# Moving the first products of a projection one pair of tiles earlier in the order of TensorE

## The reference

```python
h = rmsnorm(x, norm_mix[l])                    # x * rsqrt(mean(x*x) + eps) * g
proj = jnp.einsum('bsd,de->bse', h, w_in[l])   # [2048, 1024] x [1024, 2312]
# ... swa_sink_attention, forgetting_attention, w_out, residual, MLP, final norm
```

## Time and profile before

| what | value |
| --- | --- |
| median of 3 runs | 2398.11 us (2395.19 to 2401.05) |
| profiled execution, its time | 2394.05 us |
| its span | 2392.4 us |
| TensorE busy | 2326.6 us, 97% of the span |
| VectorE busy | 1520.1 us, 64% |
| ScalarE busy | 1154.1 us, 48% |
| GpSimd busy | 706.9 us, 30% |
| mean granted TensorE clock | 0.995 |

### The profile page before, as it was taken

One profiled execution on the slowest core, in us unless ns is written; L12 is line 12 of the kernel. 1 busy time (PEld: TensorE's weight loads), 2 busy tenths in 40 slices (PEclk: granted clock), 3 DMA queues, 4 the chain that ended last, 5 costly groups with the idle time before them and its releaser, 6 DMA issues.

```text
span 2392.4 us, 34959 instructions
## 1 busy us (share of the span) xinstructions
PE 2326.6 (97%) x11346; PEld 1934.7 (81%) x11346; DVE 1520.1 (64%) x2623; ACT 1154.1 (48%) x2226; POOL 706.9 (30%) x593
## 2 busy tenths in 40 slices
PE   7999999999999998999899999999999999999998
PEld 5888888788888886887687877888888888888887
DVE  6588873688888886566745655444465555564454
ACT  5211112788888886223545555555553233333243
POOL 2000000111111114235568764666640032120132
PEclk9999999999999999999999999999999999999999
DMA  5567765666666565766455576654457486564464
GB/s 189 215 235 278 268 242 163 180 160 156 160 157 157 152 156 169 248 218 202 170 183 163 189 286 242 202 160 152 154 190 260 165 298 234 193 219 162 138 219 160
DMA packets 253970, 469.09 MB, mean 196 GB/s; under 512 B 59336, under 2 KB 119752, under 8 KB 246032
## 3 DMA queue, kind: packets, MB, share of 16 engines
q1 hardware_dynamic: 247808, 451.11, 58.6%
q0 software_dynamic: 6048, 16.52, 2.6%
HBM read 316.13 MB, written 151.42 MB: 195 GB/s over the span
## 4 chain that ended last, share of the span: by engine, by line
PE 51%; DVE 3%; POOL 2%; issue 2%; DMA 1%; ACT 1%; SPq 0%; POOLq 0%; ACTq 0%; DVEq 0%
PE m_ps L2533 24%; PE m_ps L2556 23%; PE m_ps L1685 4%; DMA b_kept<-f_kept 1%; POOL m_mix L1548 1%; DVE f_up_lo L2389 1%; PE m_ps L2574 0%; DVE m_xn L1653 0%; DVE m_xm L1646 0%; DVE m_mix L1622 0%; ACT m_mix_hi L1585 0%; DVE keep_lo L2408 0%; POOL h_raw L1560 0%; POOL f_kept L2157 0%; DVE hop_lo L1659 0%
## 5 line engine op out<-in xcount | busy, mean ns | idle before, releaser
L2556 PE MATMUL m_ps<-keep_hi,hop_hi 128*128 128x512 f32 x880 | 342.5, 389 | 0.4 <-DVE hop_lo L2392 0.4
L2556 PE MATMUL m_ps<-keep_hi,hop_lo 128*128 128x512 f32 x880 | 342.4, 389 | 0.0
L2556 PE MATMUL m_ps<-keep_lo,hop_hi 128*128 128x512 f32 x880 | 342.3, 389 | 0.0
L2392 DVE TENSOR_TENSOR hop_lo<-h_raw,hop_hi 128x512 fp32r<-128x512 f32 x224 | 176.6, 789 | 236.8 <-ACT hop_hi L2228 236.7
L2389 DVE TENSOR_TENSOR f_up_lo<-wide_raw,f_up_hi 128x512 fp32r<-128x512 f32 x160 | 182.5, 1142 | 223.0 <-ACT f_up_hi L2223 222.9
L2228 ACT ACTIVATE hop_hi<-h_raw 128x512 fp32r<-128x512 f32 x224 | 140.8, 630 | 334.4 <-PE m_ps L2556 330.5
L958 POOL DMA_DIRECT2D o_main<-a_o x63 | 36.5, 580 | 775.2 <-ACT a_o L1326 726.6
L599 PE MATMUL p_ps_o<-p_ht_lo,p_w_hi 128*128 128x512 f32 x576 | 224.5, 390 | 0.0
L2533 PE MATMUL m_ps<-keep_hi,f_up_hi 128*128 128x512 f32 x512 | 202.8, 396 | 6.1 <-DVE f_up_lo L2389 4.7
L2533 PE MATMUL m_ps<-keep_hi,f_up_lo 128*128 128x512 f32 x512 | 201.3, 393 | 0.0
L2533 PE MATMUL m_ps<-keep_lo,f_up_hi 128*128 128x512 f32 x512 | 199.4, 390 | 0.0
(11 more groups left out here) (246 smaller groups left out, 5779.8 us busy)
## 6 DMA issues: line engine op xcount, KB each, us to landing
h_raw<-u_ops SPq DMA_DIRECT2D x224, 256.0 KB, 4.2
wide_raw<-in_w_up SPq DMA_DIRECT2D x32, 1024.0 KB, 7.2
u_ops<-f_u SPq DMA_DIRECT2D x128, 256.0 KB, 4.3
wide_raw<-in_x SPq DMA_DIRECT2D x59, 512.0 KB, 4.0
u_ops<-f_us SPq DMA_DIRECT2D x96, 256.0 KB, 2.3
proj_hi<-p_o_hi SPq DMA_DIRECT2D x17, 1024.0 KB, 6.2
proj_lo<-p_o_lo SPq DMA_DIRECT2D x17, 1024.0 KB, 8.3
h_raw<-in_w_down SPq DMA_DIRECT2D x58, 256.0 KB, 3.9
```

The lines of the kernel that those rows point to most:

```text
L2392: nc.vector.tensor_tensor(lo, a_raw[:, (m - UP) % A_RING], hi.bitcast(F32), ALU.subtract).then_inc(op_lo_done, 1)
L2556: last = nc.tensor.matmul(down_banks[b % 2][t][:], a[:, cols], w[j], start=(j == 0 and m == 0), stop=(j == FG - 1 and m == 2))
```

## The change

It does five things. `product_after_turn` becomes 3, 5, 7, 9, 11, 13 and 15 for products 0 to 6, and only product 7 stands behind all turns. `product_first(0)` asks for the low part of the first chunk's weights alone, and the others for both. On ScalarE the squares of tiles 1 to 4 are done one tile earlier relative to the high parts (squares of later tiles stay where they were), and the first two chunks' weight splits, which stood together behind tile 2, stand behind tiles 2 and 3. On VectorE the weight splits are parted likewise, and the norm of tile 4 moves behind the low part of tile 3 and the second weight split. `GATE_TILE` becomes 5. The unused squared values, which went into half of `p_o_hi0`, go into the last 256 columns of each of four pieces of `keep_hi`, where tiles 14 and 15 come later, so the wait for all squares moves from `split_first(4)` to `split_ht_hi(14)`.

```diff
-        squares = whole.raw["p_o_hi0"][:, S - D:S]
+        squares = whole.raw["keep_hi"][:].rearrange("p (k b) s -> p k (b s)", k=DK // 2)[:, :, S - 2 * P:S]
...
-        GATE_TILE = 7
+        GATE_TILE = 5
...
-        product_after_turn = {t: 2 * (t // TPB - 1) + t % TPB // 2 for t in range(TPB, ST) if t % 2}
+        product_after_turn = {2 * n + TPB - 1: n for n in range(2 * SB - 1)}
...
-                nc.scalar.activation(squares, x_in[:, t % X_RING], ACT.Square,
+                nc.scalar.activation(squares, x_in[:, t % X_RING].rearrange("p (k c) -> p k c", k=DK // 2), ACT.Square,
...
             def split_ht_hi(t):
+                if t == ST - 2:
+                    act.wait_ge(squared, ST)
...
             def split_first(n):
-                if n == 4:
-                    act.wait_ge(squared, ST)
...
             square(0)
+            square(1)
             for t in range(ST):
-                if t + 1 < ST:
-                    square(t + 1)
+                for ahead in range(t + 1, min(t + 3, ST)):
+                    if ahead == (t + 2 if ahead < X_RING else t + 1):
+                        square(ahead)
...
-                if t == 2:
-                    split_w_hi(0)
-                    split_w_hi(1)
-            for n in range(2 * SB - 3, 2 * SB - 1):
-                split_first(n)
+                if t in (2, 3):
+                    split_w_hi(t - 2)
+            split_first(2 * SB - 2)
...
-                if t + 1 < ST:
+                if t + 1 < ST and t != 3:
                     norm(t + 1)
...
-                if t == 2:
-                    split_w_lo(0)
-                    split_w_lo(1)
-            for n in range(2 * SB - 3, 2 * SB - 1):
-                split_first(n)
+                if t in (2, 3):
+                    split_w_lo(t - 2)
+                if t == 3:
+                    norm(t + 1)
+            split_first(2 * SB - 2)
...
-                pe.wait_ge(w_lo_done, 2)
+                pe.wait_ge(w_lo_done, min(n, 1) + 1)
...
-            for n in range(2 * SB - 2, 2 * SB):
-                product_first(n)
+            product_first(2 * SB - 1)
```

## The result

| | before | changed |
| --- | --- | --- |
| median | 2398.07 us (6 runs) | 2410.11 us (6 runs, 2406.09 to 2413.19) |
| ratio | | 1.0053, 95% interval 1.0043 to 1.0063 |
| span of the profiled execution | 2392.4 us | 2409.7 us |
| product 0 ends | 33.51 us | 27.81 us |
| product 7 ends | 82.45 us | 94.32 us |

What follows compares the result with a forecast made beforehand. TensorE was taken to run without slack behind the first eight products. Product 0's end 28.3 + chain 62.1 + clock 5.5 = 95.9 against 82.45 us, 13.4 us later: 2411.5 us, range 2404 to 2417 us.

Steps and rivals of the forecast that it cites:

- What bounds: TensorE behind the first eight products: runs without slack, so any shift of product 7's end (82.45 us) is handed on.
- The start of product 0: First products: product 0 starts at 20.35 instead of 26.97 us and ends at 28.3 instead of 33.51, 5.2 us gained.
- The stalls: Ahead of products 2, 4 and 6: TensorE waits for a tile's low part, new idle times of 4.56, 4.56 and 2.30 us.
- The clock: TensorE behind the three stalls: clock falls to half rate, costing 2.1, 2.1 and 1.3 us, 5.5 us in all.
- first rival: At products 2, 4 and 6: stalls come but the clock holds; shift 7.9 or 5.4 us, 2403.5 to 2406 us; chance 0.20.
- The second: First products: the clock costs its upper bound, 2.8 us for all three stalls; 18.7 us later, 2416.8 us; chance 0.10.
- The third: First products: earlier start outweighs stalls if these total under 3.4 us; -2.0 us, 2396 us; chance 0.04.
- The fourth: First products: faster splits, held clock, stalls of 5 to 6 us against 3.4 us gained; 2 us, 2400 us; chance 0.06.
- The edits costed at nothing: Squares' new destination, the wait for all squares at tile 14, loads of x and chunk 2's waits: no cost.

Runs made afterwards that it cites:

- e6_change_again: The changed kernel timed and profiled once more, nothing altered: 2410.59 us, ratio 1.0057 to the kernel before.
- e2: The changed kernel with square and norm of tiles 8 and 12 moved behind the splits of tiles 7 and 11: 2401.29 us, ratio 1.0026 to the kernel before.
- e3_filled: The changed kernel with useless matmuls (18, 18, 8) in the stalls ahead of products 2, 4 and 6: 2404.36 us, ratio 1.0030 to the kernel before.
- e7_relaid_near: The changed kernel with products 0 to 5 behind turns 3, 5, 8, 10, 12, 15, squares and norms at most three tiles ahead: 2399.60 us, ratio 1.0010.
- e1_old_places: The changed kernel with the products' old places and the gate behind tile 7, other edits kept: ratio 0.9999 to the kernel before.
- e5_relaid: The changed kernel with products 0 to 5 behind turns 3, 5, 8, 10, 12, 15, squares and norms up to four tiles ahead: 2401.33 us, ratio 1.0023.
- e4: The changed kernel with only product 0 one pair earlier, products 0 to 5 behind turns 3, 7, 9, 11, 13, 15: 2400.29 us, ratio 1.0014.

## Why the prediction was right

**What bounds.** TensorE was at its limit behind product 7, and the shift of product 7's end was carried on unchanged for the next 340 us: it is 11.87 us at 82 us and still 11.87 us at 425 us of the kernel before, matmul by matmul. The median moved 12.0. The prediction went further and said that every stretch behind would take as long as before. In the profiles that did not hold: the shift is 11.97 us at 485, 15.8 at 500 and 17.3 us at the end, and 16.5 at the end of e6_change_again. That the median shows next to nothing of it in the first set of runs is not explained, so the closeness of 12.0 to 11.87 is in part luck.

**The start of product 0.** Forecast at 20.35, measured 20.62; the turn of tile 3 forecast from 16.6 to 17.7, measured 16.57 to 18.2. Its end, forecast at 28.3 between bounds of 25.8 and 30.7, came at 27.81. The clock's part in it was over-sized: 14 slow matmuls were forecast and 8 came, since by the matmuls' distances the clock fell only at about 21.2 us, inside the product, and was back by about 24.6.

**The stalls.** Products 2, 4 and 6 start 6.29, 6.29 and 4.03 us behind the end of the product before; forecast 6.33, 6.33 and 4.07. (The idle times read 4.38 and 2.13 instead of 4.56 and 2.30, because the profile gives the two turns 1.91 us, where the prediction took 1.77.) That the tile's split could be read off the kernel before, at a place where nobody waited for it, is what carried the forecast. e2 shows that the reason given, the next tile's norm and its wait ahead of the low part, was the right one, together with that tile's square, for 2.3 of the 4.4 us.

**The clock.** This was the one clearly mis-sized term. Forecast 2.1, 2.1 and 1.3 us, 5.5 in sum. Against the 5.58 us that a product behind a stall takes at the full clock, products 2 and 4 took 2.40 and 1.63 us more and product 6 nothing, 4.0 in sum, and filling the stalls won the same 4.0. The clock did not fall behind the third stall. The 0.14 us between 5.58 and 5.44 are no matter of the clock; the sum left them out three times. With 1.5 us too much for the clock, product 0's end 0.5 us sooner, and 0.4 us for this left out, 95.9 comes to 94.3, against 94.32 us measured.

The evidence for this term was thinner than the prediction had it. It took the gap of 4.10 us in the kernel before as the case of a long gap that lowers the clock, also against its first rival. But that gap began at 22.96 - 4.10 = 18.86 us, and the mean of 0.79 from 18.5 to 19.0 us puts the fall at about 18.8 us, an estimate: the clock fell no later than the gap began, behind the shorter gaps of 0.42 and 1.91 us, and that gap can't have caused it. So no row of the kernel before showed a fall by a gap of that length. That the clock would fall at the two long stalls came true, but this reading did not show it; the stalls of 4.38 us and e3_filled did.

**The rivals.** The first (the clock holds) fell in the profile, where it read 0.50 behind both long stalls. The second (the upper bound everywhere) would have needed 2.8 us three times; it was 2.4, 1.6 and nothing. The third, a faster kernel, needed stalls under 3.4 us in sum; e7_relaid_near has three of 0.79, 2.4 us, beside the gate's wait, which the kernel before had too, and its first products do end 0.6 us sooner. That agrees with the point, but only another order reaches it, and the time of the whole shows no gain. The fourth needed stalls of 5 to 6 us in sum; they were 10.9.

**The edits costed at nothing.** e1_old_places has all of them and the old places, and its ratio is 0.9999.

The Trainium skill's rule that idle time between bursts sends the engine back to half rate ("TensorE: Matmul & The Clock Gate", HAM oscillation — how this bites in real kernels) agrees with the two long stalls, at which the clock went to 0.50. Its other sentence, that the count of slow matmuls varies from run to run (Part 1, What's actually happening), these runs show: product 0 took 27.81 - 20.62 = 7.19 us in the changed kernel, with 8 slow matmuls, and 7.97 us in e3_filled, with 12, with the same instructions ahead of it.

## What to carry to other kernels

When an engine works in a fixed order, count for each wait how many items of other work lie between the producer's trigger and the wait; moving a consumer earlier by one item takes that cover away at every wait of its kind, while the gain is had once. Read the producer's latency from the trace at a place where nobody waits for it yet, and look at what stands ahead of the awaited result on its engine, here a norm that could as well stand behind it. Running work further ahead helps only as far as its transfers have landed.

## What the runs showed of the hardware

Idle times of about 2 us on TensorE let the clock fall in some cases and not in others: 2.06 us (yes) and 2.06 us (no) within one execution of e2_norm_behind, 1.89 (yes) and 2.02 (no) in e5_relaid, 2.13 (no) in the changed kernel. The four waits of 2.1 to 2.5 us for the `decay` load were all followed by a fall. All idle times of 3.5 us and more on a TensorE that had been busy at the full clock were too (3.51 in e4, 4.85 in e1, 4.37 or 4.38 twice in each profile of the changed kernel), and those of 0.79 us in e5 and e7 were not. The fall came within the idle time or up to about 1.6 us behind its end (e5_relaid: idle until 41.56, clock still 1.00 from 42 to 43 us and 0.56 from 43 to 44).

A fall behind a stall cost the product 1.6 to 2.5 us, counted from 5.58 us: 1.59 in e5, 1.61 in e2, 1.63 and 2.40 in the changed kernel, 1.64 and 2.51 when it was run again.
